# Head totals in a decoder layer: a rounded part and a remainder in place of full fp32 operands

## The chip, the cores and the metric

The kernel runs on one NeuronCore of a Trainium2 chip. The metric is the device time of one execution in microseconds (us). The engines work side by side and meet at semaphores: TensorE (PE) multiplies and writes PSUM banks, VectorE (DVE) and ScalarE (ACT) do elementwise work, GpSimd (POOL) and SyncE (SP) mostly start DMA transfers. Each engine takes its instructions in the order in which they are written, so whatever stands behind a wait on its engine waits too.

## What is computed

One inference step of one decoder layer for 256 prompt tokens and 8 requests of 4 tokens each, 288 token columns in all. The part that the change touches is the RWKV-7 branch, cut to its core:

```
kk = heads(k * k_k)
kk = kk * rsqrt(max(sum(kk * kk, axis=-1), 1e-24))              # total over a head of 64 channels
... S = S * w + (S a) b + v k  per token, y = S r ...
mean = mean(y, axis=-1)                                          # total over a head
var  = mean(square(y - mean), axis=-1)                           # total over a head
y = (y - mean) * rsqrt(var + GN_EPS) * lnx_w + lnx_b
bonus = sum(r_h * k_h * r_k, axis=-1) * v_h                      # total over a head
out = (y + bonus) * g
```

Around it stand the large products `n @ w_in`, the gates, `p_rw`, `p_att`, `w_o`, `w_up` and `w_down`, all in fp32.

## The kernel before

**The stream.** Nearly all of TensorE's time goes to the large products. Their weights come in units of 16 blocks (a block is a 128x128 tile of weights, a unit is 1 MB, loaded by one DMA). To reach fp32 accuracy each weight tile is made into a rounded part `w_hi` (a ScalarE copy to the type fp32r) and a remainder `w_lo` (a VectorE subtraction), and the activations into `x_split` in the same way. A block is then three matmuls of 128x288: `w_lo` by the activations' rounded part (L621), `w_hi` by their remainder (L622), `w_hi` by their rounded part (L623). A unit n may start when the semaphore `w_split` says that its `w_lo` is done and `unit_out` says that the bank of the unit before last is read.

**The pairs.** The 16 heads are done two at a time in 8 pairs (a loop over 7 and a last one that is written out). A pair is a chain of small fp32 matmuls with VectorE and ScalarE steps between them. Where TensorE would have to wait for such a step, `fill(count)` puts in so many blocks of the gate weights. A pair has four units, 64 blocks, to fill with; `fill` counts them on, and the first block of each unit waits for that unit's `w_lo`. In order, a pair takes 39 blocks up to the point at which y is made, and the tail of a pair is this:

```python
                mm(BK[5][:, 0:N], head_ones, YS[:], start=True, stop=True).then_inc(sem("y_mean"), 1)
                if not last:
                    kk_sum(it + 2)
                fill(4)
                pe.wait_ge(sem("y_sq"), v)
                mm(BK[5][:, 0:N], head_ones, YQ[:], start=True, stop=True).then_inc(sem("y_var"), 1)
                if not last:
                    log_decay(it + 2)
                fill(6)
                if not last:
                    bonus_mm(it + 2)
                fill(KT * 4 - pos[0])
```

The pair's first three units use up blocks 0 to 47; block 48, the first of the fourth unit, lies in `fill(6)`. `head_ones` is a 128x128 matrix that adds the 64 channels of each of the two heads. Four totals use it, each as one fp32 matmul of 128x288: the mean of y (L1116), its variance (L1121), and for the next pair the norm of kk (`kk_sum`, L862) and the bonus (`bonus_mm`, L875).

**VectorE in the tail.** In written order: the last states `state(c)`, the grown request state (L2253), the copy of y for the requests (L2256), `mix_prev` for v, the request state by its decay (L2262), y less its mean (L2265), `kk_max` (L2046), two quarters of the fourth unit's `w_lo` (L579), `k_mixed` for the next pair (L2062, L2063), the other two quarters (L579; the last one raises `w_split`), then `head` for the next pair: a reciprocal (L2074) and ten short steps up to `ar_ready`, which TensorE waits for at the start of the next pair (L905), and last the `w_lo` of the next pair's first unit (L567).

**The last pair** has no next pair to prepare: after its four `w_lo` quarters VectorE goes on with the reciprocal of the standard deviation (L2108), the norm, the gate, the `w_lo` of the first unit of the projection, and `o_split` (L2306), for which TensorE waits at the projection's first block.

**Ahead of the pairs** the same steps stand once for pair 0, with `fill_cols` in the place of `fill`: `kk_square` on ScalarE (L1459), `kk_sum(1)`, `log_decay(1)`, `bonus_mm(1)`. On VectorE `streamed(FILL_FIRST)`, the `w_lo` of a unit, stands ahead of `kk_max(1)`.

**The start.** `first_units` begins with four units in step, a quarter of each at a time. The first blocks need quarter 0 of the first unit as `w_hi` (L1258) and `w_lo` (L1777), and the first activations as rounded part (L1247) and remainder (L1769).

## Time and profile before

| | |
|---|---|
| time of three runs | 1776.01, 1778.01, 1780.81 us; median 1778.01 |
| the profiled execution | 1776.88 us, its span 1775.3 us |
| mean granted TensorE clock | 0.996 of full |
| TensorE busy | 1758.8 us, 99% of the span |
| VectorE busy | 1120.7 us, 63% |
| ScalarE busy | 759.6 us, 43% |
| the pairs | from about 360 us to 711 us |

Times in the views are microseconds from the start of the span. A row of a timeline has the start, the time up to the end of the last one, the engine, the line, the operation, its output and inputs, and how many instructions were merged; in brackets stands the idle time just before and what ended it. PEld is the load of a weight tile, which goes on beside the matmuls. Matmuls are pipelined: one row's time is that from its start to its modelled end, and the pace is the distance between starts. An fp32 matmul stands as two records, one of the fp32r type as one record.

### The profile page before, as it was taken

The page shows a single profiled execution, that of the slowest core. Times are in us where ns is not written, and L with a number is a line of the kernel's source. Part 1 is how long each engine was busy: PE and PEld are TensorE (multiplying, and loading weights), DVE is VectorE, ACT ScalarE, POOL GpSimd, SP SyncE. Part 2 cuts the span into 40 slices and gives each one's busy share as a digit, 9 for nine tenths or more (in the row PEclk, how much of TensorE's full clock was granted, in tenths as well). Part 3 has the DMA queues.
Part 4 walks back from the last instruction along what each step waited for, and adds up shares of the span by engine and source line. Part 5 has one row for each costly group of instructions (what it writes and reads, how often), then busy time and mean ns, then how long its engine had stood idle before and what let it go on. Part 6 is the DMA issues. An engine that isn't in the chain of part 4 may idle for free.

```text
span 1775.3 us, 40657 instructions
## 1 busy us (share of the span) xinstructions
PE 1758.8 (99%) x16482; PEld 1708.2 (96%) x16482; DVE 1120.7 (63%) x2015; ACT 759.6 (43%) x1059; POOL 53.8 (3%) x103
## 2 busy tenths in 40 slices
PE   9999999999999999999999999999999999999997
PEld 9999899999999998999999999999999999999997
DVE  7764864667777777665566666666666665444443
ACT  6456444555555554333443333333333333333332
POOL 2500000000000000000000000000000000000000
PEclk9999999999999999999999999999999999999998
DMA  7644344433333332644454444444444444555553
GB/s 285 220 165 165 124 162 157 143 115 118 112 112 117 112 111 103 220 166 170 171 220 163 157 164 158 168 161 167 164 165 165 165 165 167 172 169 175 170 169 134
DMA packets 51697, 283.47 MB, mean 160 GB/s; under 512 B 7248, under 2 KB 11856, under 8 KB 25776
## 3 DMA queue, kind: packets, MB, share of 16 engines
q1 hardware_dynamic: 43488, 260.32, 41.9%
q10 hardware_dynamic: 3888, 12.59, 1.9%
q0 software_dynamic: 4256, 9.65, 1.8%
q8 instruction: 46, 0.75, 0.2%
q14 instruction: 19, 0.16, 0.0%
HBM read 274.26 MB, written 8.27 MB: 159 GB/s over the span
## 4 chain that ended last, share of the span: by engine, by line
PE 96%; DVE 3%; DMA 0%; ACT 0%; issue 0%; DVEq 0%; ACTq 0%
PE bank L621 30%; PE bank L623 28%; PE bank L622 28%; PE bank L945 1%; PE bank L985 1%; DVE w_lo L567 1%; DVE scores L1939 1%; PE bank L642 0%; PE bank L643 0%; PE bank L644 0%; DMA w_raw<-in_w_in 0%; PE bank L905 0%; DVE max L1906 0%; PE bank L852 0%; PE bank L800 0%; PE bank L817 0%
## 5 line engine op out<-in xcount | busy, mean ns | idle before, releaser
L621 PE MATMUL bank<-x_split,w_lo 128*128 128x288 f32 x2880 | 872.8, 303 | 2.8 <-DVE w_lo L567 2.1
L622 PE MATMUL bank<-x_split,w_hi 128*128 128x288 f32 x2880 | 849.6, 295 | 0.0
L623 PE MATMUL bank<-x_split,w_hi 128*128 128x288 f32 x2880 | 847.2, 294 | 0.0
L587 ACT ACTIVATE w_hi<-w_raw 128x2048 fp32r<-128x2048 f32 (+1 forms) x262 | 468.7, 1789 | 591.8 <-PE bank L623 579.1
L567 DVE TENSOR_TENSOR w_lo<-w_raw,w_hi 128x2048 fp32r<-128x2048 f32 (+1 forms) x238 | 503.8, 2117 | 283.2 <-ACT w_hi L587 282.9
L621 PEld LDWEIGHTS bank<-x_split,w_lo 128*128 128x128 f32 x2880 | 540.3, 188 | 18.0 <-issue 8.2
L622 PEld LDWEIGHTS bank<-x_split,w_hi 128*128 128x128 f32 x2880 | 541.0, 188 | 2.6 <-issue 1.5
L623 PEld LDWEIGHTS bank<-x_split,w_hi 128*128 128x128 f32 x2880 | 542.2, 188 | 0.0
L621 PE MATMUL bank<-act_split,w_lo 128*128 128x288 f32 x704 | 208.5, 296 | 0.0
L622 PE MATMUL bank<-act_split,w_hi 128*128 128x288 f32 x704 | 207.7, 295 | 0.0
L623 PE MATMUL bank<-act_split,w_hi 128*128 128x288 f32 x704 | 207.0, 294 | 0.0
L623 PEld LDWEIGHTS bank<-act_split,w_hi 128*128 128x128 f32 x704 | 132.6, 188 | 0.0
L622 PEld LDWEIGHTS bank<-act_split,w_hi 128*128 128x128 f32 x704 | 132.2, 188 | 0.0
L621 PEld LDWEIGHTS bank<-act_split,w_lo 128*128 128x128 f32 x704 | 131.9, 187 | 0.2 <-DVE w_lo L567 0.2
L621 PE MATMUL bank<-merged_split,w_lo 128*128 128x288 f32 x256 | 75.9, 296 | 0.0
L622 PE MATMUL bank<-merged_split,w_hi 128*128 128x288 f32 x256 | 75.5, 295 | 0.0
L623 PE MATMUL bank<-merged_split,w_hi 128*128 128x288 f32 x256 | 75.3, 294 | 0.0
L2397 DVE TENSOR_TENSOR conv<-bank,h_rstd 128x288 f32<-128x288 f32 x44 | 20.2, 458 | 67.9 <-PE bank L623 67.9
L579 DVE TENSOR_TENSOR w_lo<-w_raw,w_hi 128x512 fp32r<-128x512 f32 x96 | 62.1, 683 | 1.1
L1320 ACT ACTIVATE cols<-bank 128x256 f32<-128x256 f32 x40 | 15.4, 385 | 90.5 <-PE bank L623 90.5
L2380 DVE TENSOR_TENSOR gate_ext<-bank,h_rstd 128x256 f32<-128x256 f32 x44 | 18.7, 425 | 55.0 <-PE bank L623 55.0
L623 PEld LDWEIGHTS bank<-merged_split,w_hi 128*128 128x128 f32 x256 | 48.2, 188 | 0.0
(396 smaller groups left out, 1544.2 us busy)
## 6 DMA issues: line engine op xcount, KB each, us to landing
w_raw<-in_w_up SPq DMA_DIRECT2D x88, 1024.0 KB, 4.8
w_raw<-in_w_in SPq DMA_DIRECT2D x47, 1024.0 KB, 4.9
w_raw<-in_w_down SPq DMA_DIRECT2D x64, 704.0 KB, 4.1
w_raw<-in_w_gate SPq DMA_DIRECT2D x32, 1024.0 KB, 4.8
w_raw<-in_w_p SPq DMA_DIRECT2D x16, 1024.0 KB, 4.9
w_raw<-in_w_o SPq DMA_DIRECT2D x16, 1024.0 KB, 4.8
h<-in_x ACTq DMA_DIRECT2D x1, 2304.0 KB, 11.2
h_spill<-h ACTq DMA_DIRECT2D x1, 2304.0 KB, 9.3
```

Source lines behind the costliest of these rows:

```text
L567: eng.tensor_tensor(WLO[:, slot, 0:kt], WRAW[:, slot, 0:kt], WHI[:, slot, 0:kt].bitcast(F32), ALU.subtract).then_inc(sem("w_split"), 1)
L579: ins = dve.tensor_tensor(WLO[:, slot, k], WRAW[:, slot, k], WHI[:, slot, k].bitcast(F32), ALU.subtract)
L587: actv(WHI[:, slot, 0:kt], WRAW[:, slot, 0:kt], ACT.Copy).then_inc(sem("w_hi"), 3 if isinstance(n, int) and n == 2 else 1)
L621: mm(out, wl, hi, start=first and k == ks[0], stop=False, skip_group_check=True)
L622: mm(out, w, lo, start=False, stop=False, skip_group_check=True)
L623: ins = mm(out, w, hi, start=False, stop=last and k == ks[-1], skip_group_check=True)
L945: ins = mm(BK[bank][q, u * w:(u + 1) * w], lhs[q, u], rhs[q, u], start=True, stop=True)
L985: return mm(BK[banks[par]][halves[e], c0:c0 + CH], lhs, rhs, start=start, stop=False, skip_group_check=True)
L1320: actv(tile[:, 1:1 + SEQ], BK[j % 2][:, 0:SEQ], ACT.Copy)
L1939: ins = V.scalar_tensor_tensor(acc, src, w, acc if i or par else causal[qt], ALU.mult, ALU.add)
L2380: V.tensor_tensor(gx[:, 2:2 + SEQ], BK[0][:, 0:SEQ], HRSTD[:, 0:SEQ], ALU.mult)
L2397: st.done(V.tensor_tensor(c[:, 0:N], BK[1][:, 0:N], HRSTD[:], ALU.mult))
```

## The change

- Each of the four totals is made by `head_sum` from two fp32r matmuls, the remainder first, then the rounded part, with a ones matrix `HONES` of the type fp32r. The operands are new: `SQS` (squares of k), `YSS` (y, and then its squares) and `RKS` (the bonus product).
- The rounded parts of the squares of k, of y and of its squares are made on ScalarE by a second activation; their remainders on VectorE by a subtraction. Both parts of the bonus product are made on VectorE, a copy (CAST) and a subtraction.
- In the tail of a pair `kk_sum` goes ahead of the mean, and `fill(4)` and `fill(6)` become `fill(6)` and `fill(5)`.
- VectorE: the grown request state goes ahead of the state of chunk 3; `kk_lo` stands behind that state, and in the part ahead of the pairs it stands ahead of `streamed(FILL_FIRST)`. The map of chunk 3 becomes a tile of its own, 128x64.
- At the start the first unit's first two blocks put the products with `w_hi` first and those with `w_lo` after them, and the first two activations are made ahead of the weights.

```diff
--- before.py
+++ after.py
@@ -390,3 +390,5 @@
     LO = m("l_off", [P, 2, 2 * BL])
-    MTB = m("chunk_map", [P, NCH - 1, P])
+    HONES = m("head_ones_r", [P, P], F32R)
+    MTB = m("chunk_map", [P, NCH - 2, P])
+    MT3 = m("chunk_map_3", [P, CH])
     MLS = region(vv_at)("m_low_s", [NS, 2, NS])
@@ -859,5 +874,10 @@
 
+            def head_sum(bank, split):
+
+                mm(BK[bank][:, 0:N], HONES[:], split[:, 1, :], start=True, stop=False, skip_group_check=True)
+                return mm(BK[bank][:, 0:N], HONES[:], split[:, 0, :], start=False, stop=True, skip_group_check=True)
+
             def kk_sum(v):
-                pe.wait_ge(sem("kk_sq"), v)
-                mm(BK[3][:, 0:N], head_ones, SQK[:], start=True, stop=True).then_inc(sem("kk_sum"), 1)
+                pe.wait_ge(sem("kk_sq"), 2 * v)
+                head_sum(3, SQS).then_inc(sem("kk_sum"), 1)
 
@@ -1113,13 +1133,13 @@
 
-                pe.wait_ge(sem("y"), v)
-                pe.wait_ge(sem("y_cols"), v)
-                mm(BK[5][:, 0:N], head_ones, YS[:], start=True, stop=True).then_inc(sem("y_mean"), 1)
                 if not last:
+                    pe.wait_ge(sem("y_cols"), 2 * v - 1)
                     kk_sum(it + 2)
-                fill(4)
-                pe.wait_ge(sem("y_sq"), v)
-                mm(BK[5][:, 0:N], head_ones, YQ[:], start=True, stop=True).then_inc(sem("y_var"), 1)
+                pe.wait_ge(sem("y"), 3 * v - 1)
+                head_sum(5, YSS).then_inc(sem("y_mean"), 1)
+                fill(6)
+                pe.wait_ge(sem("y"), 3 * v)
+                head_sum(5, YSS).then_inc(sem("y_var"), 1)
                 if not last:
                     log_decay(it + 2)
-                fill(6)
+                fill(5)
                 if not last:
@@ -1261,5 +1281,5 @@
             actv(ROOT[:, 0:1], NORMS[:, 0, 0:1], ACT.Copy)
+            first_hi(0, 2, "x_in0")
             act.wait_ge(sem("w_first_in"), 16)
             first_weights(0, [0])
-            first_hi(0, 2, "x_in0")
             first_hi(2, 4, "x_in0b")
@@ -1458,3 +1478,5 @@
                 act.wait_ge(sem("rkv"), v)
-                actv(SQK[:], RKV[:, 1, :], ACT.Square, scale=PRM[:, PR_KK:PR_KK + 1]).then_inc(sem("kk_sq"), 1)
+                for dst in (SQK[:], SQS[:, 0, :]):
+                    ins = actv(dst, RKV[:, 1, :], ACT.Square, scale=PRM[:, PR_KK:PR_KK + 1])
+                ins.then_inc(sem("kk_sq"), 1)
 
@@ -1544,2 +1566,5 @@
                 ins.then_inc(sem("y_cols"), 1)
+                act.wait_ge(sem("y"), 3 * v - 2)
+                act.wait_ge(sem("y_cols"), 2 * v - 1)
+                actv(YSS[:, 0, :], YS[:], ACT.Copy).then_inc(sem("y_cols"), 1)
                 if not last:
@@ -1548,3 +1573,5 @@
                 act.wait_ge(sem("y_centred"), v)
-                actv(YQ[:], YS[:], ACT.Square).then_inc(sem("y_sq"), 1)
+                for dst in (YQ[:], YSS[:, 0, :]):
+                    ins = actv(dst, YS[:], ACT.Square)
+                ins.then_inc(sem("y_sq"), 1)
                 if not last:
@@ -1806,5 +1833,6 @@
 
-            first_weights(0, [0])
             dve.wait_ge(sem("norms_in"), 16)
-            first_lo(0, 4)
+            first_lo(0, 2)
+            first_weights(0, [0])
+            first_lo(2, 4)
             first_weights(0, [1, 2, 3])
@@ -2043,2 +2071,7 @@
 
+            def kk_lo(v):
+
+                dve.wait_ge(sem("kk_sq"), 2 * v - 1)
+                V.tensor_tensor(SQS[:, 1, :], SQK[:], SQS[:, 0, :].bitcast(F32), ALU.subtract).then_inc(sem("kk_sq"), 1)
+
             def kk_max(v):
@@ -2062,4 +2095,5 @@
                 st.done(V.scalar_tensor_tensor(KP[:], KP[:], 1.0, RKV[:, 1, :], ALU.add, ALU.mult))
-                V.scalar_tensor_tensor(RKR[:], RKV[:, 0, :], PRM[:, PR_RK:PR_RK + 1], KP[:], ALU.mult,
-                                       ALU.mult).then_inc(sem("rkr"), 1)
+                st.done(V.scalar_tensor_tensor(RKR[:], RKV[:, 0, :], PRM[:, PR_RK:PR_RK + 1], KP[:], ALU.mult, ALU.mult))
+                st.done(V.tensor_copy(RKS[:, 0, :], RKR[:]))
+                V.tensor_tensor(RKS[:, 1, :], RKR[:], RKS[:, 0, :].bitcast(F32), ALU.subtract).then_inc(sem("rkr"), 1)
 
@@ -2230,8 +2264,6 @@
                 state(0)
-                for e, h in enumerate(halves):
-                    V.tensor_tensor(MTB[h, 0::2, e * HD:(e + 1) * HD], BK[7][h, P:2 * P].rearrange("p (u f) -> p u f", u=2),
-                                    spread(eye_ch[h], 1, [CH, 2, CH]), ALU.add)
-                for e, h in enumerate(halves):
-                    ins = V.tensor_tensor(MTB[h, 1, e * HD:(e + 1) * HD], BK[6][h, P + CH:2 * P], eye_ch[h], ALU.add)
-                ins.then_inc(sem("map"), 1)
+                for c, src in ((1, BK[7][:, P:P + CH]), (2, BK[6][:, P + CH:2 * P])):
+                    for e, h in enumerate(halves):
+                        V.tensor_tensor(MTB[h, c - 1, e * HD:(e + 1) * HD], src[h], eye_ch[h], ALU.add)
+                V.tensor_tensor(MT3[:], BK[7][:, P + CH:2 * P], eye_ch, ALU.add).then_inc(sem("map"), 1)
                 rv = AR[:, 1, :].rearrange("p (c f) -> p c f", f=CH)
@@ -2247,9 +2279,12 @@
                         mix_prev(it + 1, 0)
+                    if c == 3:
+                        dve.wait_ge(sem("state_s_mm"), v)
+                        for r in range(2):
+                            half = SIN[:, 4 * r:4 * r + 4, :]
+                            ins = V.tensor_tensor(half, half, BK[(5, 2)[r]][:, 0:256].rearrange("p (b f) -> p b f", f=HD), ALU.add)
+                        ins.then_inc(sem("s_grown"), 1)
                     dve.wait_ge(sem("state_mm"), v * 3 - 3 + c)
                     state(c)
-                dve.wait_ge(sem("state_s_mm"), v)
-                for r in range(2):
-                    half = SIN[:, 4 * r:4 * r + 4, :]
-                    ins = V.tensor_tensor(half, half, BK[(5, 2)[r]][:, 0:256].rearrange("p (b f) -> p b f", f=HD), ALU.add)
-                ins.then_inc(sem("s_grown"), 1)
+                if not last:
+                    kk_lo(it + 2)
                 dve.wait_ge(sem("y_mm"), v)
@@ -2260,5 +2295,7 @@
                     dve.sem_inc(sem("v_mixed"), 1)
+                dve.wait_ge(sem("y_cols"), 2 * v)
+                V.tensor_tensor(YSS[:, 1, :], YS[:], YSS[:, 0, :].bitcast(F32), ALU.subtract).then_inc(sem("y"), 1)
                 dve.wait_ge(sem("s_grown"), v)
                 V.tensor_tensor(SIN[:], SIN[:], spread(PC[:, NCH:], 2, [P, DB, HD]), ALU.mult).then_inc(sem("state_s_done"), 1)
-                dve.wait_ge(sem("y"), v)
+                dve.wait_ge(sem("y"), 3 * v - 1)
                 dve.wait_ge(sem("y_mean"), v)
@@ -2267,2 +2304,4 @@
                     kk_max(it + 2)
+                dve.wait_ge(sem("y_sq"), v)
+                V.tensor_tensor(YSS[:, 1, :], YQ[:], YSS[:, 0, :].bitcast(F32), ALU.subtract).then_inc(sem("y"), 1)
                 for part in range(2):
@@ -2285,2 +2324,4 @@
             dve.sem_inc(sem("v_mixed"), 1)
+            st.done(V.tensor_copy(HONES[:], head_ones))
+            kk_lo(1)
             streamed(FILL_FIRST)
```

**TensorE, tail of a pair.** `bank<-y,main_consts` is a head total of before; `bank<-y_split,head_ones_r` is one of the two matmuls of a total of the change, and `waits` names the semaphores of a row. Left out ("...") are only rows of blocks. Before:

```order
L1116 MATMUL bank<-y,main_consts 128x288 [waits y_cols,y]
L862 MATMUL bank<-squares_k,main_consts 128x288 [waits kk_sq]
...
L1121 MATMUL bank<-y_sq,main_consts 128x288 [waits y_sq]
L870 MATMUL bank<-main_consts,decay_tok 128x130 [waits g_sb,decay_tok]
...
L887 REGISTER_ALU
L621 MATMUL bank<-x_split,w_lo 128x288 [waits unit_out,w_split]
...
L875 MATMUL bank<-r_k_rk,main_consts 128x288 [waits rkr]
```

With the change:

```order
L881 REGISTER_ALU [waits y_cols]
L877 MATMUL bank<-squares_k_split,head_ones_r 128x288 [waits kk_sq]
L878 MATMUL bank<-squares_k_split,head_ones_r 128x288
...
L877 MATMUL bank<-y_split,head_ones_r 128x288 [waits y]
...
L890 MATMUL bank<-main_consts,decay_tok 128x130 [waits g_sb,decay_tok]
...
L907 REGISTER_ALU
L627 MATMUL bank<-x_split,w_lo 128x288 [waits unit_out,w_split]
...
L877 MATMUL bank<-r_k_rk_split,head_ones_r 128x288 [waits rkr]
```

Between the mean and the row that waits for `w_split` (block 48) stood nine blocks and stand nine blocks (four and five before, six and three now), with the variance and `log_decay` two blocks later among them. Behind that row one block stood ahead of the bonus, and two stand there now.

**VectorE, tail of a pair**, from the copy of y to the reciprocal of the next pair's head. Before:

```order
L2256 COPY y<-bank 128x32 [waits y_mm]
...
L2262 TENSOR_TENSOR state_s<-state_s,chunk_decay 128x512 [waits dve_step,s_grown]
L2265 SCALAR_TENSOR_TENSOR y<-bank,y 128x288 [waits y_mean,y]
L2046 TENSOR_SCALAR squares_k<-bank 128x288 [waits kk_sum]
L579 TENSOR_TENSOR w_lo<-w_raw,w_hi 128x512 [waits w_hi]
L579 TENSOR_TENSOR w_lo<-w_raw,w_hi 128x512
L2062 SCALAR_TENSOR_TENSOR k_mixed<-k_mixed,rkv 128x288 [waits k_part,rkv]
L2063 SCALAR_TENSOR_TENSOR r_k_rk<-rkv,pair_params,k_mixed 128x288 [waits dve_step]
L579 TENSOR_TENSOR w_lo<-w_raw,w_hi 128x512 x2
L2074 RECIPROCAL squares_k<-squares_k 128x288 [waits kk_norm]
```

With the change:

```order
L2302 SCALAR_TENSOR_TENSOR y<-bank,y 128x288 [waits y_mean,y]
L2079 TENSOR_SCALAR squares_k<-bank 128x288 [waits kk_sum]
L2306 TENSOR_TENSOR y_split<-y_sq,y_split 128x288 [waits y_sq]
L585 TENSOR_TENSOR w_lo<-w_raw,w_hi 128x512 [waits w_hi]
L585 TENSOR_TENSOR w_lo<-w_raw,w_hi 128x512
L2095 SCALAR_TENSOR_TENSOR k_mixed<-k_mixed,rkv 128x288 [waits k_part,rkv]
L2096 SCALAR_TENSOR_TENSOR r_k_rk<-rkv,pair_params,k_mixed 128x288 [waits dve_step]
L2097 CAST r_k_rk_split<-r_k_rk 128x288 [waits dve_step]
L2098 TENSOR_TENSOR r_k_rk_split<-r_k_rk,r_k_rk_split 128x288 [waits dve_step]
L585 TENSOR_TENSOR w_lo<-w_raw,w_hi 128x512 x2
L2108 RECIPROCAL squares_k<-squares_k 128x288 [waits kk_norm]
```

A subtraction that waits for ScalarE's squares now stands ahead of the first two quarters of `w_lo`, and a copy and a subtraction, each behind a wait of VectorE for itself, ahead of the last two.

## Rows read from the trace of the kernel before

**Rows 1.** The page's first part: busy time, share of span, instructions.

```profile
PE 1758.8 (99%) x16482; PEld 1708.2 (96%) x16482; DVE 1120.7 (63%) x2015; ACT 759.6 (43%) x1059; POOL 53.8 (3%) x103
```

**Rows 2.** Windows: length, busy time and instructions of PE, PEld, DVE, ACT, POOL; PEclk.

```profile
11.00:12.80 1.80, 1.80 (x7) 1.80 (x8) 1.80 (x4) 1.80 (x5) 0.00 (x0) 0.50 0.93 383
391.00:435.10 44.10, 44.10 (x746) 39.79 (x745) 35.15 (x93) 23.20 (x50) 2.20 (x4) 1.00 0.32 113
1000.00:1700.00 700.00, 700.00 (x5250) 699.77 (x5249) 401.44 (x606) 252.85 (x225) 0.00 (x0) 1.00 0.48 166
```

**Rows 3.** Timeline of TensorE in the tail of a pair.

```profile
391.28 0.65 PE L1116 MATMUL bank<-y,main_consts 128*128 128x288 f32 x2
...
391.76 0.65 PE L862 MATMUL bank<-squares_k,main_consts 128*128 128x288 f32 x2
...
393.84 0.65 PE L1121 MATMUL bank<-y_sq,main_consts 128*128 128x288 f32 x2
...
396.99 0.30 PE L621 MATMUL bank<-x_split,w_lo 128*128 128x288 f32 x1
...
403.87 0.38 PE L905 MATMUL bank<-main_consts,b_t 128*128 128x128 f32 x2
```

**Rows 4.** Timeline of VectorE in the same tail.

```profile
392.04 0.46 DVE L2265 SCALAR_TENSOR_TENSOR y<-bank,y 128x288 f32<-128x288 f32 x1 [1.14 <-PE bank L1116]
...
392.82 1.28 DVE L579 TENSOR_TENSOR w_lo<-w_raw,w_hi 128x512 fp32r<-128x512 f32 x2
...
394.51 0.52 DVE L2063 SCALAR_TENSOR_TENSOR r_k_rk<-rkv,pair_params,k_mixed 128x288 f32<-128x288 f32 x1
394.95 1.29 DVE L579 TENSOR_TENSOR w_lo<-w_raw,w_hi 128x512 fp32r<-128x512 f32 x2
...
398.32 0.52 DVE L2075 SCALAR_TENSOR_TENSOR kk_unit<-rkv,pair_params,squares_k 128x288 f32<-128x288 f32 x1
398.88 0.46 DVE L2076 SCALAR_TENSOR_TENSOR a_gate<-a_gate,kk_unit 128x288 f32<-128x288 f32 x1
...
400.79 0.42 DVE L2102 TENSOR_TENSOR k_t<-k_mixed,decay_exp 128x256 f32<-128x256 f32 x1
```

**Rows 5.** Timeline of ScalarE in the same tail.

```profile
392.53 0.44 ACT L1549 ACTIVATE y_sq<-y 128x288 f32<-128x288 f32 x1 [0.55 <-DVE y L2265]
392.88 0.51 ACT L1450 ACTIVATE decay_tok<-decay_tok 128x384 f32<-128x384 f32 x1
```

**Rows 6.** Groups of instructions by shape (count, busy us, mean ns), VectorE.

```profile
L2032 DVE TENSOR_SCALAR cols<-cols 128x288 f32<-128x288 f32 x1 | 0.3, 311 | 0.0
```

**Rows 7.** Timelines of the part ahead of the pairs.

```profile
341.28 0.53 ACT L1459 ACTIVATE squares_k<-rkv,pair_params 128x288 f32<-128x288 f32 x1
341.42 2.29 DVE L567 TENSOR_TENSOR w_lo<-w_raw,w_hi 128x2048 fp32r<-128x2048 f32 x1 [0.21 <-ACT w_hi L587]
350.13 2.28 DVE L567 TENSOR_TENSOR w_lo<-w_raw,w_hi 128x2048 fp32r<-128x2048 f32 x1
342.10 0.65 PE L862 MATMUL bank<-squares_k,main_consts 128*128 128x288 f32 x2
353.29 0.30 PE L621 MATMUL bank<-x_split,w_lo 128*128 128x288 f32 x1
```

**Rows 8.** Timeline of the last pair's tail.

```profile
698.88 0.45 ACT L1543 ACTIVATE y<-bank 128x128 f32<-128x128 f32 x2 [1.72 <-PE bank L985]
699.66 0.72 PE L1116 MATMUL bank<-y,main_consts 128*128 128x288 f32 x2
700.86 2.48 DVE L579 TENSOR_TENSOR w_lo<-w_raw,w_hi 128x512 fp32r<-128x512 f32 x4
710.88 0.37 PE L621 MATMUL bank<-x_split,w_lo 128*128 128x288 f32 x1
```

**Rows 9.** Timeline of TensorE at the start.

```profile
8.43 0.37 PE L642 MATMUL bank<-x_split,w_lo 128*128 128x288 f32 x1 [1.84 <-DVE x_split L1769]
...
10.99 0.61 PE L642 MATMUL bank<-x_split,w_lo 128*128 128x288 f32 x1 [0.28 <-DVE w_lo L1777]
```

More of the change, by code:

```diff
@@ L191 @@
 ATT_STEPS = [("sample", 0), (0, 0), (0, 1), (1, 0), (1, 1), ("sample", 1)]
-PAIR_STEPS = 16
+PAIR_STEPS = 18
 TOKEN_TILES = (0, P, N - P)
@@ L398, in build @@
     RKR = m("r_k_rk", [P, N])
+    RKS = m("r_k_rk_split", [P, 2, N], F32R)
+    YSS = m("y_split", [P, 2, N], F32R)
+    assert m.at <= inv_at + 3 * size_of([P, 4, CH])
+    SQS = region(r0)("squares_k_split", [P, 2, N], F32R)
     m = region(big)
@@ L631, in first_units @@
                     for u in range(FIRST):
+                        out = BK[first_bank(u)][:, 0:N]
+                        if s == 0 and u == 0:
+                            pe.wait_ge(sem("w_part_hi"), 1)
+                            for k in range(2):
+                                pe.wait_ge(sem("x_split"), k + 1)
+                                mm(out, WHI[:, 0, k], XN[:, 0, k], start=k == 0, stop=False, skip_group_check=True)
+                                mm(out, WHI[:, 0, k], XN[:, 1, k], start=False, stop=False, skip_group_check=True)
                         if s < 2 and u < 3:
@@ L635, in first_units @@
                             pe.wait_ge(sem("w_split"), s + 1)
-                        out = BK[first_bank(u)][:, 0:N]
-                        for k in range(4):
+                        if s == 0 and u == 0:
+                            for k in range(2):
+                                mm(out, WLO[:, 0, k], XN[:, 0, k], start=False, stop=False, skip_group_check=True)
+                        for k in range(2 if s == 0 and u == 0 else 0, 4):
                             t = 4 * s + k
@@ L874, in bonus_mm @@
                 pe.wait_ge(sem("rkr"), v)
-                mm(BK[4][:, 0:N], head_ones, RKR[:], start=True, stop=True).then_inc(sem("bonus_mm"), 1)
+                head_sum(4, RKS).then_inc(sem("bonus_mm"), 1)
             def pair(it, last=False):
@@ L1097, in pair @@
                 for e, h in enumerate(halves):
-                    ins = grown(grow, 0, 1, MTB[h, 2, e * HD:(e + 1) * HD], ST[h, 2, :], e, 1)
+                    ins = grown(grow, 0, 1, MT3[h], ST[h, 2, :], e, 1)
                 ins.then_inc(sem("state_mm"), 1)
```

2 lines of the change are left out of this document (1 added, 1 removed).

## The prediction

> **What bounds the kernel now.** I read the page first: TensorE is busy 99% of the span [rows 1], so time is won only where it gets less to do, and lost wherever it waits. The windows come next. In the pure stream it starts 5250 matmuls in 700 us, 0.133 us each, 0.40 us a block; in a pair it is busy through the whole window, while VectorE has 35.15 and ScalarE 23.20 of 44.10 us [rows 2]. A pair takes (699.66 - 391.28) / 7 = 44.05 us from one mean to the next [rows 3, 8]. So the share of busy time says that VectorE has room, but the question is where in the pair it has it. For that I read the three engines' timelines over the tail of a pair [rows 3 to 5]: block 48 starts at 396.99 us, and the last quarter of its `w_lo` ends at 394.95 + 1.29 = 396.24 us. The fourth unit has 0.75 us to spare, much less than the average suggests.
>
> **What TensorE saves.** A total in fp32 takes 391.76 - 391.28 = 0.48 us [rows 3]. Two fp32r matmuls of the same shape at the stream's pace take 2 x 0.133 = 0.27 us. Each total saves 0.21 us; four in a pair save 0.86 us and two in the last pair 0.43 us. All blocks are done in either order, and the map of chunk 3 keeps the shape of its matmuls: nothing there.
>
> **When TensorE reaches block 48.** Nine blocks lie between the mean and block 48 in both kernels, and three totals besides: 396.99 - 3 x 0.21 = 396.35 us. The other 0.21 us is saved by the bonus, behind it.
>
> **When the `w_lo` of block 48 is ready.** I follow VectorE, on the clock of the same tail.
> - The mean now follows the norm of kk and ends with a short matmul: starts 391.55 and 391.68, end 0.30 later, 391.97, against about 391.93 before. L2265 starts at 392.08 instead of 392.04 [rows 4].
> - ScalarE squares y at 392.57. Its next activation could start 392.88 - 392.53 = 0.35 us later [rows 5], so the second square runs from 392.92 and takes 0.44: 393.36. VectorE has by then ended `kk_max` (392.08 + 0.37 + 0.46 = 392.91) and stands still. At 393.40 it makes the remainder. A VectorE instruction on 128x288 lasts 0.46 us and lets the next start some 0.09 us ahead of its end: the quarters start at 393.77, 0.95 us later than the 392.82 of before [rows 4].
> - L2063 starts 394.51 - 392.82 = 1.69 us after the first quarter: 395.46. The next quarters came 0.44 us after that. Now the copy has to wait until L2063 has written, and L2075 to L2076 shows what such a wait makes of a 0.52 us instruction: 0.56 us [rows 4]. Copy and subtraction follow: 0.35 + 0.37. The last two quarters start at 395.46 + 0.56 + 0.35 + 0.37 = 396.74 and end at 398.03. TensorE goes on at 398.08.
> - The copy's 0.31 us is that of L2032, a one-input instruction of this width from SBUF to SBUF [rows 6]. It is the nearest row. The upper bound is the 0.46 us of L2265, 0.15 us more a pair; nothing of this width is below L2032.
>
> The Trainium skill ("VectorE: DVE Perf Modes") says that fp32 instructions with one SBUF input can run at twice the rate of those with two, and the 0.31 against 0.46 us agree with it; it does not say whether writing fp32r keeps this. By the one the forecast would stand, by the other it would be 1 us higher.
>
> **So TensorE waits 398.08 - 396.35 = 1.73 us at block 48**, a wait that does not exist now, and 0.86 us of it is paid by the shorter totals: **+0.87 us a pair**, 7 pairs, **+6.1 us**. With the copy at 0.46, with 0.1 more for ScalarE's hand-over, it is 1.1 a pair (7.7 us); with 0.1 us less than I count, 0.75 (5.3 us). Behind the wait on TensorE stand two blocks, the bonus, and the rest of the unit. The bonus needs the remainder of its operand, ready at about 396.8: hidden by the wait at block 48; without it, TensorE would reach the bonus near 397.1 and still not wait. The head of the next pair shifts by about 1.7 us on VectorE, but TensorE reaches L905 at 403.87 + 0.87 = 404.74, and `ar_ready`, raised at 400.79 + 0.42 = 401.21 before [rows 4], is there at 402.9. The `w_lo` behind it takes 2.3 us [rows 7] and ends about 405.5; the block that needs it stands behind all transposes and the first products of the next pair. ScalarE is 0.35 us later and has idle time in each pair [rows 2].
>
> **Hidden edits.** `kk_lo` and y's remainder (0.46 us each) fall into the 1.14 us in which VectorE waited for the mean [rows 4]. `kk_lo` hangs on ScalarE's two squares and y's remainder on ScalarE's copy; both have a good microsecond until the matmuls that read them at 391.28 and 391.55. The grown request state moves into a gap ahead of the last state. The map costs VectorE one short instruction more, about 0.1 us, under two blocks of stream. Without these covers each would cost at most its own length a pair.
>
> **The last pair.** It has no norm of kk or LoRA products ahead of its mean as cover. ScalarE has y at 698.88 + 0.45 = 699.33; a rounded part (0.44) and a remainder (0.45) more with their hand-overs: 700.30, and TensorE, there at 699.66, waits until 700.35. The mean is then short, and L2265 starts about 0.42 us later than before. Two squares and the remainder put the four quarters at 702.60 instead of 700.86, and what VectorE does next (reciprocal, norm, gate, `w_lo`, `o_split`) goes on 1.74 us later. TensorE reaches the projection's first block about 0.85 us later than before and finds it not ready: it starts at 710.88 + 1.74 [rows 8]. **+1.7 us** (0.85 if the first block of the projection hangs on TensorE alone now, to 2.0).
>
> **Ahead of the pairs.** ScalarE squares k at 341.28; with a second square it ends at about 342.22, VectorE's remainder at 342.71. TensorE reaches the total at 342.10 [rows 7] and waits 0.66 us for it. The `w_lo` behind `kk_lo` starts 1.2 us later, and with the copy and subtraction of the bonus (0.79) the `w_lo` of 350.13 + 2.28 = 352.41 ends at 354.40 instead. Its unit starts at 353.29 [rows 7], now 353.29 + 0.66 - 0.43 = 353.52, and waits 0.9 us. In all **+1.2 us** (0.4 to 1.4).
>
> **The start.** The first four products with `w_hi` run in a stretch in which TensorE waited until 8.43. But the second unit starts when its own `w_lo` is there, at 10.99, as before [rows 9]; the weights come from a DMA that isn't moved. What can be won is the half clock of 1.2 GHz that rows show here (0.50 in 11.0 to 12.8 us [rows 2], after TensorE had stood still for 1.84 us): up to 0.9 us if the clock rises earlier; if it stays low longer through the new gap, 1 us is lost. I take **-0.4 us**.
>
> **Sum.** 6.1 + 1.7 + 1.2 - 0.4 = +8.6 us against the profiled execution's 1776.88 us: 1785.5. That execution is 1.13 us below the median of 1778.01, so I forecast **1786.6 us**, 0.48% slower.
>
> **The rivals.**
> 1. *The stall is short and the sum stays within 0.3%.* For it: the start may give 0.9 us, the copy and hand-overs have bounds of 0.1 us, and the wait ahead of the pairs and in the last pair rests on margins of a few tenths. All low ends together: 5.3 + 0.85 + 0.4 - 0.9 = +5.7; with a pair at 0.65 instead of 0.75, +5: 1783. Against it: five low ends at a time. 0.13.
> 2. *The clock falls at each stall.* A gap of 1.84 us at the start was followed by a stretch at 0.50 of the clock. In its part from 11.0 to 12.8 us TensorE started 7 matmuls, where the stream's pace gives 13.5: 6.5 x 0.133 = 0.9 us lost there, and with what lies ahead of 11.0 I estimate 1.4 us [rows 2, 9]. The new gap in a pair is nearly as long (1.6 to 1.7 us). If it did the same in every pair: 7 x 1.4 = 9.8 more, 1796 us; in two or three pairs, 1790. Against it: TensorE is busy without a gap ahead of it, and at the start it was not. 0.15. The Trainium skill ("TensorE: Matmul & The Clock Gate", HAM oscillation) says that idle gaps in a loop can throw TensorE back to half clock again and again, and this start is such a case; no gap of this length in the middle of a busy stretch is in this trace.
> 3. *The gain comes through: faster.* The totals save 32 x 0.21 = 6.8 us, 1771 us. It decides on one point: the `w_lo` of block 48 must be ready by 396.35. Even without the change it is ready at 396.28, so VectorE may lose no more than 0.07 us ahead of it, and I count 1.8 us: the squares' hand-over 0.95, copy and subtraction 0.84. Only a wrong reading of which unit `fill(5)` enters would do it. 0.04.
> The forecast's own case has 0.68, with a range of 1784 to 1790.
>
> **Numbers.** A measurement of this kernel tells about 0.3% (5.3 us) from no change, so slower by more than that begins at 1783.3. Slower has the forecast's case and rival 2, 0.82 with a little of their low ends taken off; within 0.3% 0.14; faster 0.04. The range leaves out the gain and the clock falling in every pair, and takes in part of rivals 1 and 2: 1782 to 1793 us.
>
> **What the changed profile would show.** TensorE's waits: a row for blocks of the stream, released by VectorE's `w_lo` quarters, some 1.6 us long and seven times; none in the pairs would refute me. In the timeline two records 0.13 us apart for each total, and the wait three blocks behind `log_decay`, two ahead of the bonus; at any other block I have misread its place. VectorE idle 0.45 us ahead of the remainder of y's squares. Mean to mean 44.9 us instead of 44.05. The first block of the projection near 1.7 us later after the last mean. What would make me wrong is a copy or a hand-over much shorter than its bounds, a clock below 1.00 in the pairs' windows, or a second wait in the pair that I hold to be covered, at L905 above all.

## The result and the profile after

| kernel | median us | range, runs | ratio to before [95%] |
|---|---|---|---|
| before | 1776.57 | 1776.01 to 1780.81, 7 | |
| changed | 1785.54 | 1784.27 to 1788.55, 7 | 1.0052 [1.0042, 1.0061] |

The change costs 8.97 us, 0.52%. The profiled execution of the changed kernel took 1788.55 us (span 1787.0), 3.0 us above its own median; most of these 3 us lie at the start, as told below.

The chain of reading is the same as before the change: the page first, then the list of waits, then the timelines of the tail. The page of the changed kernel, first part and the group of the stream's `w_lo` blocks (the last two numbers are the idle time ahead of the group and what ended most of it):

```profile
PE 1754.4 (98%) x16482; PEld 1704.2 (95%) x16482; DVE 1136.7 (64%) x2064; ACT 768.5 (43%) x1083; POOL 53.8 (3%) x103
...
L627 PE MATMUL bank<-x_split,w_lo 128*128 128x288 f32 x2880 | 870.1, 302 | 15.7 <-DVE w_lo L585 11.5
```

TensorE is busy 4.4 us less than in [rows 1] and yet the span is 11.7 us longer: it stands still. The waits of TensorE say where (waited in total, times, longest, us):

```profile
PE bank L627 <- DVE w_lo L585: 11.5, 8, 1.6
...
PE bank L657 <- DVE w_lo L573: 1.8, 1, 1.8
PE bank L643 <- ACT w_hi L1278: 1.7, 1, 1.7
PE bank L627 <- DVE x_split L2347: 0.7, 1, 0.7
PE bank L877 <- DVE squares_k_split L2075: 0.6, 1, 0.6
PE bank L877 <- DVE y_split L2297: 0.6, 1, 0.6
```

Its first row is the forecast wait at block 48: 7 times 1.57 us, and 0.48 us once in the last pair. TensorE's timeline in the tail of a pair, against [rows 3]:

```profile
394.37 0.51 PE L877 MATMUL bank<-squares_k_split,head_ones_r 128*128 128x288 f32 x1
394.72 0.30 PE L878 MATMUL bank<-squares_k_split,head_ones_r 128*128 128x288 f32 x1
394.86 0.29 PE L877 MATMUL bank<-y_split,head_ones_r 128*128 128x288 f32 x1
...
399.25 0.29 PE L627 MATMUL bank<-x_split,w_lo 128*128 128x288 f32 x1
...
401.38 0.40 PE L627 MATMUL bank<-x_split,w_lo 128*128 128x288 f32 x1 [1.57 <-DVE w_lo L585]
...
401.89 0.29 PE L627 MATMUL bank<-x_split,w_lo 128*128 128x288 f32 x1
...
402.28 0.30 PE L877 MATMUL bank<-r_k_rk_split,head_ones_r 128*128 128x288 f32 x1
...
665.50 0.29 PE L877 MATMUL bank<-y_split,head_ones_r 128*128 128x288 f32 x1
```

The block at 399.25 is the last of the third unit. A block takes 0.40 us, so block 48 would have started at 399.65; it starts at 401.38, 1.73 us later. (The view's 1.57 is counted from the modelled end of the block before. By starts each wait is 0.16 us longer than the view says, and starts are what adds up.) From the first mean to the seventh are (665.50 - 394.86) / 6 = 45.11 us. Two blocks behind the wait the bonus follows without one. The block behind the wait takes longer: its successor starts at 401.89, 0.51 us later and not 0.40.

VectorE's timeline of the same tail, against [rows 4], and the two squares of ScalarE:

```profile
395.40 0.46 DVE L2302 SCALAR_TENSOR_TENSOR y<-bank,y 128x288 f32<-128x288 f32 x1 [0.78 <-PE bank L878]
395.77 0.45 DVE L2079 TENSOR_SCALAR squares_k<-bank 128x288 f32<-128x288 f32 x1
396.70 0.46 DVE L2306 TENSOR_TENSOR y_split<-y_sq,y_split 128x288 fp32r<-128x288 f32 x1 [0.48 <-ACT y_split L1575]
397.07 1.29 DVE L585 TENSOR_TENSOR w_lo<-w_raw,w_hi 128x512 fp32r<-128x512 f32 x2
398.77 0.52 DVE L2096 SCALAR_TENSOR_TENSOR r_k_rk<-rkv,pair_params,k_mixed 128x288 f32<-128x288 f32 x1
399.32 0.31 DVE L2097 CAST r_k_rk_split<-r_k_rk 128x288 fp32r<-128x288 f32 x1
399.66 0.46 DVE L2098 TENSOR_TENSOR r_k_rk_split<-r_k_rk,r_k_rk_split 128x288 fp32r<-128x288 f32 x1
400.04 1.29 DVE L585 TENSOR_TENSOR w_lo<-w_raw,w_hi 128x512 fp32r<-128x512 f32 x2
```

```profile
395.89 0.45 ACT L1575 ACTIVATE y_sq<-y 128x288 f32<-128x288 f32 x1 [0.60 <-DVE y L2302]
396.24 0.43 ACT L1575 ACTIVATE y_split<-y 128x288 fp32r<-128x288 f32 x1
```

Before the change the first pair of quarters started 0.78 us behind the centring (392.82 - 392.04 in [rows 4]); now 397.07 - 395.40 = 1.67. From the first pair of quarters to the second were 2.13 us; now 400.04 - 397.07 = 2.97. So the handover of the squares costs 0.89 us and the split of the bonus's operand 0.84 us (2.97 - 2.13). The last quarter ends at 401.33, and TensorE goes on 0.05 us later.

The windows, as in [rows 2] (length, busy time and instructions of PE, PEld, DVE, ACT, POOL; PEclk is the number behind POOL's):

```profile
394.86:440.08 45.22, 43.65 (x748) 39.53 (x747) 37.07 (x99) 24.46 (x54) 2.20 (x4) 1.00 0.32 110
400.00:404.00 4.00, 2.62 (x19) 2.62 (x20) 3.93 (x6) 3.99 (x8) 0.00 (x0) 1.00 0.63 208
11.00:12.80 1.80, 1.80 (x15) 1.80 (x14) 1.80 (x5) 1.63 (x4) 0.00 (x0) 1.00 1.00 392
```

VectorE is busy 37.07 of 45.22 us, 82%, in a pair in which TensorE waits for it. The clock of the pairs is 1.00, also in the 4 us around the wait. At the start it is 1.00 where [rows 2] have 0.50. But it falls later. These windows lie ahead of and behind the wait of 1.84 us that ends at 23.60 us (its row stands below):

```profile
10.80:21.70 10.90, 10.90 (x83) 10.72 (x81) 6.98 (x15) 7.76 (x15) 0.00 (x0) 1.00 0.94 338
25.00:28.00 3.00, 3.00 (x14) 3.00 (x14) 2.49 (x3) 3.00 (x4) 0.00 (x0) 0.50 0.85 339
```

TensorE was busy without a gap for more than 10 us, stood for 1.84 us, and about 1.3 us after it went on it ran at 0.50 for some 3 us: 13 matmuls at 0.24 us and not 0.133, 1.4 us lost on top of the wait.

The part ahead of the pairs, the last pair and the start, against [rows 7], [rows 8] and [rows 9], TensorE and (for `y`) ScalarE:

```profile
344.89 0.40 PE L877 MATMUL bank<-squares_k_split,head_ones_r 128*128 128x288 f32 x1 [0.59 <-DVE squares_k_split L2075]
356.57 0.40 PE L627 MATMUL bank<-x_split,w_lo 128*128 128x288 f32 x1 [0.65 <-DVE w_lo L573]
```

```profile
708.78 0.45 ACT L1565 ACTIVATE y<-bank 128x128 f32<-128x128 f32 x2 [1.83 <-PE bank L1005]
710.31 0.41 PE L877 MATMUL bank<-y_split,head_ones_r 128*128 128x288 f32 x1 [0.58 <-DVE y_split L2297]
722.56 0.37 PE L627 MATMUL bank<-x_split,w_lo 128*128 128x288 f32 x1 [0.71 <-DVE x_split L2347]
```

```profile
10.30 0.40 PE L657 MATMUL bank<-x_split,w_lo 128*128 128x288 f32 x1 [0.61 <-DVE w_lo L1804]
23.60 0.40 PE L657 MATMUL bank<-x_split,w_lo 128*128 128x288 f32 x1 [1.84 <-DVE w_lo L573]
```

Ahead of the pairs the total of k's squares waits 0.59 us for its remainder, and the unit at 356.57 0.65 us for its `w_lo`. In the last pair 722.56 - 708.78 = 13.78 us lie between ScalarE's y and the projection's first block, where [rows 8] give 710.88 - 698.88 = 12.00: +1.78. At the start the second unit begins 0.69 us earlier than in [rows 9], at full clock; at 23.60 TensorE then stands for 1.84 us.

What start and preparation cost together is read from two landmarks of TensorE, one behind the start and one ahead of the first norm and mean in the loop. Before:

```profile
71.67 0.38 PE L662 MATMUL bank<-main_consts,cols 128*128 128x128 f32 x2
390.79 0.65 PE L858 MATMUL bank<-cols,lora 128*128 128x288 f32 x2
```

With the change:

```profile
73.68 0.38 PE L677 MATMUL bank<-main_consts,cols 128*128 128x128 f32 x2
394.10 0.65 PE L873 MATMUL bank<-cols,lora 128*128 128x288 f32 x2
```

The first is 2.01 us later, the second 3.31.

### The profile page after: what moved, and what is told of

Its sections match the earlier page's. It is cut to its first block, busy times and chain, and to the rows that moved or that the text cites. A ratio compares the mean times of both kernels' runs of the same rounds, so it can differ in the third digit from the quotient of the medians.

```text
span 1787.0 us, 40776 instructions
## 1 busy us (share of the span) xinstructions
PE 1754.4 (98%) x16482; PEld 1704.2 (95%) x16482; DVE 1136.7 (64%) x2064; ACT 768.5 (43%) x1083; POOL 53.8 (3%) x103
## 4 chain that ended last, share of the span: by engine, by line
PE 91%; DVE 6%; issue 1%; ACT 1%; DMA 1%; DVEq 0%; ACTq 0%
PE bank L627 29%; PE bank L629 27%; PE bank L628 27%; PE bank L965 1%; DVE w_lo L573 1%; PE bank L1005 1%; DVE w_lo L585 1%; DVE scores L1967 1%; DMA w_raw<-in_w_in 1%; PE bank L925 0%; DVE max L1934 0%; PE bank L867 0%; PE bank L815 0%; PE bank L832 0%; PE bank L657 0%
## 5 line engine op out<-in xcount | busy, mean ns | idle before, releaser
L627 PE MATMUL bank<-x_split,w_lo 128*128 128x288 f32 x2880 | 870.1, 302 | 15.7 <-DVE w_lo L585 11.5
L593 ACT ACTIVATE w_hi<-w_raw 128x2048 fp32r<-128x2048 f32 (+1 forms) x262 | 468.9, 1790 | 595.1 <-PE bank L629 583.9
```

What stands on the lines that cost most here:

```text
L593: actv(WHI[:, slot, 0:kt], WRAW[:, slot, 0:kt], ACT.Copy).then_inc(sem("w_hi"), 3 if isinstance(n, int) and n == 2 else 1)
L627: mm(out, wl, hi, start=first and k == ks[0], stop=False, skip_group_check=True)
```

## The experiments

Each is timed against the kernel before. a_order, a_bonus, a_squares and b_start ran on one chip (before: 1776.26 us, 29 runs), the others on a second one (1776.11, 18 runs). No runs of the changed kernel stand beside them, so a difference between two of these kernels, or to the changed kernel's 1785.54 us, rests on the kernel before as the common measure; the ratios say how well. "Pair" is the distance between the second and the third execution of ScalarE's y copy in the profile: 44.19 us before (432.98 to 477.17), 45.11 in the changed kernel (437.26 to 482.37).

| kernel | median us (range, runs) | ratio [95%] | pair us | wait at block 48, us |
|---|---|---|---|---|
| a_order | 1775.63 (1774.68 to 1778.34, 11) | 0.9999 [0.9990, 1.0008] | 43.72 | none |
| a_bonus | 1780.99 (1780.29 to 1783.20, 7) | 1.0031 [1.0019, 1.0042] | 44.48 | 0.73 |
| a_squares | 1778.52 (1777.61 to 1780.30, 11) | 1.0013 [1.0004, 1.0022] | 44.21 | 0.46 |
| b_start | 1776.74 (1774.36 to 1777.72, 11) | 1.0001 [0.9992, 1.0010] | 44.18 | none |
| a_ends | 1782.87 (1781.90 to 1783.26, 5) | 1.0037 [1.0024, 1.0050] | 45.09 | 1.57 |
| a_nostart | 1786.59 (1785.07 to 1787.41, 5) | 1.0055 [1.0043, 1.0068] | 45.11 | 1.57 |
| c_fill | 1772.85 (1771.64 to 1777.59, 12) | 0.9982 [0.9974, 0.9991] | 43.34 | none |
| c_ends | 1770.55 (1769.42 to 1771.57, 6) | 0.9966 [0.9955, 0.9978] | 43.34 | none |

**a_order** moves only VectorE's work in the pair: the quarters of the fourth unit ahead of the squares' remainder (one of them ahead of its wait) and ahead of the bonus's operand.

```diff
-                dve.wait_ge(sem("y_sq"), v)
-                V.tensor_tensor(YSS[:, 1, :], YQ[:], ...).then_inc(sem("y"), 1)
-                for part in range(2):
-                    split_part(dve, n + 3, 1, part)
-                if not last:
-                    k_mixed(it + 2)
-                for part in range(2, 4):
-                    split_part(dve, n + 3, 1, part)
+                split_part(dve, n + 3, 1, 0)
+                dve.wait_ge(sem("y_sq"), v)
+                V.tensor_tensor(YSS[:, 1, :], YQ[:], ...).then_inc(sem("y"), 1)
+                for part in range(1, 4):
+                    split_part(dve, n + 3, 1, part)
+                if not last:
+                    k_mixed(it + 2)
```

> The changed kernel with one move on VectorE: in the tail of a pair one quarter of the fourth unit's w_lo goes ahead of the remainder of y's squares, and the other three go ahead of k_mixed, so that all four stand ahead of the bonus product's copy and subtraction. No work is added or left out. If the loss is the wait for that w_lo at block 48 (my theory): the quarters end near 395.7 on the clock of the prediction, TensorE comes at 396.35, the wait of 1.6 us a pair goes, and a wait of about 0.3 us at the bonus takes its place; 7 x 1.3 and 0.6 in the last pair: about 10 us less than the changed kernel, near 1775.5. If the loss is the added work as such, or a slower clock or slower matmuls of the head totals, wherever VectorE does it (rival): within 1 us of the changed kernel's 1785.5.

All operations are still there, and 9.9 us of the time are gone (9.4 by the ratios, 1.0052 less 0.9999). The wait at block 48 has left the list; in its place stands a short one of the bonus for its remainder. The row of the list of waits, and the same wait in TensorE's timeline with the last block ahead of it:

```profile
PE bank L877 <- DVE r_k_rk_split L2098: 1.4, 7, 0.2
```

```profile
398.01 0.29 PE L627 MATMUL bank<-x_split,w_lo 128*128 128x288 f32 x1
...
398.77 0.40 PE L877 MATMUL bank<-r_k_rk_split,head_ones_r 128*128 128x288 f32 x1 [0.20 <-DVE r_k_rk_split L2098]
```

By starts it is 398.77 - (398.01 + 0.40) = 0.36 us. The pair should be 0.86 shorter and 0.36 longer than 44.19, 43.69; it is 43.72. With the same work on VectorE and the same two squares on ScalarE the stall at block 48 is gone: it came from what stood ahead of the `w_lo` quarters, not from the sum of the work. The kernel is only level with the one before, since the bonus waits now and the parts outside the loop still lose.

**a_bonus** takes the bonus back to one fp32 matmul; the copy and the subtraction are left out on VectorE.

```diff
-                head_sum(4, RKS).then_inc(sem("bonus_mm"), 1)
+                mm(BK[4][:, 0:N], head_ones, RKR[:], start=True, stop=True).then_inc(sem("bonus_mm"), 1)
...
-                st.done(V.tensor_copy(RKS[:, 0, :], RKR[:]))
-                V.tensor_tensor(RKS[:, 1, :], RKR[:], RKS[:, 0, :].bitcast(F32), ALU.subtract).then_inc(sem("rkr"), 1)
```

> The changed kernel with the bonus total alone back in fp32 (no copy and no subtraction on VectorE for it). By my theory VectorE's last two quarters come 0.79 us earlier, the wait at block 48 falls from 1.6 to 0.8 us, and the fp32 total behind it costs 0.21: 7 x -0.58 = -4.1, and -0.4 ahead of the pairs: near 1781. By the rival, that TensorE's own time is all that counts, it gets 8 x 0.21 = 1.7 us slower: 1787.

```profile
PE bank L627 <- DVE w_lo L585: 5.6, 8, 0.7
```

The wait falls by 1.57 - 0.73 = 0.84 us, the whole price of the split as forecast, and the pair is 0.63 us shorter than the change's: 0.84 less the 0.21 that the bonus now costs TensorE again. The time, 1780.99 us, is that of the theory (1781) and not that of the rival (1787).

**a_squares** takes the total of y's squares back: one square on ScalarE, no remainder on VectorE, one fp32 matmul.

```diff
-                pe.wait_ge(sem("y"), 3 * v)
-                head_sum(5, YSS).then_inc(sem("y_var"), 1)
+                pe.wait_ge(sem("y_sq"), v)
+                mm(BK[5][:, 0:N], head_ones, YQ[:], start=True, stop=True).then_inc(sem("y_var"), 1)
...
-                dve.wait_ge(sem("y_sq"), v)
-                V.tensor_tensor(YSS[:, 1, :], YQ[:], YSS[:, 0, :].bitcast(F32), ALU.subtract).then_inc(sem("y"), 1)
```

> The changed kernel with the variance alone back in fp32 (one square on ScalarE, no remainder on VectorE). By my theory the quarters come 0.95 us earlier and TensorE comes 0.21 us later to block 48: wait 0.45 us instead of 1.6, net -0.95 a pair, -6.6, and -1.0 in the last pair, where the chain of VectorE sets the start of the projection: near 1778. By the rival that TensorE's own time is all that counts: 8 x 0.21 slower, 1787.

The wait is 0.46 us, seven times (0.47 once). By starts it is 0.62, and the three totals that stay short pay 3 x 0.21: the pair is 44.21 us, that of before. The 2.3 us that the kernel still loses lie outside the looped pairs: 1.3 ahead of them, and 1.0 in the last pair, where 13.01 us lie between ScalarE's y and the projection, against 12.00.

**b_start** is the kernel before with the change's start alone; **a_nostart** is the change with the start of before.

```diff
-            act.wait_ge(sem("w_first_in"), 16)
-            first_weights(0, [0])
             first_hi(0, 2, "x_in0")
+            act.wait_ge(sem("w_first_in"), 16)
+            first_weights(0, [0])
...
-            first_weights(0, [0])
             dve.wait_ge(sem("norms_in"), 16)
-            first_lo(0, 4)
+            first_lo(0, 2)
+            first_weights(0, [0])
+            first_lo(2, 4)
```

and on TensorE the first unit's products with `w_hi` of its first two blocks ahead of those with `w_lo`.

> The kernel before with the change of the start alone. I forecast -0.4 us (from -0.9 to +1.0) for it: the second unit is bound by its weights, and only the half clock at 9.7 to 12.8 us can be won. In the profile of the changed kernel the stretch ran at full clock, but TensorE then waited 1.8 us at 23.6 us for the third quarter's w_lo, whose weights had come late. If that late landing belongs to the changed start, this kernel is 1 to 2 us slower than before; if it is chance, it is within 0.5 us.

> The changed kernel with the start as it was before. The start alone, on the kernel before, was within 0.5 us, since TensorE gets 1.6 us ahead and then waits for the third quarter's w_lo. So 1785.5 within 1 us. If the late landing seen in the changed profile is typical for the changed start, this is 2 us faster: 1783.5.

The windows of both (a_nostart, then b_start), and the waits of TensorE ahead of the first unit and in it:

```profile
9.70:12.80 3.10, 3.10 (x14) 3.10 (x14) 3.10 (x7) 2.85 (x8) 0.00 (x0) 0.50 0.97 403
```

```profile
9.70:12.80 3.10, 2.47 (x19) 2.24 (x18) 2.74 (x6) 3.07 (x7) 0.00 (x0) 1.00 0.95 398
```

```profile
PE bank L648 <- DVE x_split L1787: 1.8, 1, 1.8
```

```profile
PE bank L637 <- ACT w_hi L1267: 1.1, 1, 1.1
```

The clock follows the start: 0.50 with the old order and its gap of 1.8 us, 1.00 with the new one, whose gap (1.1 us in b_start) lies earlier. The other seven kernels with the new start show 1.00 in this window as well. The times do not: b_start's interval spans 0.9 in 1000 either way, 1.6 us, and those of a_nostart and of the change overlap. Neither the forecast 0.4 us nor zero is excluded. a_nostart was expected within 1 us of the changed kernel's 1785.54 and came 1.05 above it.

The traces show what decides it. TensorE's lead from the full clock lasts until it wants the third quarter's `w_lo` near 23 us, and that hangs on when the weights have landed. ScalarE's first rounding of that quarter began at 17.29 us before, at 17.50 in b_start, 18.43 in a_nostart, 18.64 in a_order and 19.30 in the changed kernel:

```profile
19.30 1.92 ACT L593 ACTIVATE w_hi<-w_raw 128x2048 fp32r<-128x2048 f32 x1 [2.96 <-issue]
```

The load of this quarter was issued at 12.17 us before and took 5.0 us to land; in the changed kernel it was issued earlier, at 11.48, and took 7.8. Over all ten kernels it was issued between 11.3 and 12.2 us and took 5.0 to 7.8 us. TensorE waited for the quarter 1.84 us in the changed kernel, 1.1 in a_order, and not at all in b_start and a_nostart.

The landmark behind the start (L662 and its like, 71.67 us before) says what each start was worth in its one profiled execution:

| start | kernel: rounding of the third quarter from, landmark (us) |
|---|---|
| old | before: 17.29, 71.67; a_nostart: 18.43, 71.48 |
| new, landed early | b_start: 17.50, 70.58; a_squares: 17.78, 70.81; a_ends: 17.84, 70.89 |
| new, later | a_bonus: 18.16, 72.41; c_ends: 18.40, 71.43; a_order: 18.64, 71.68; changed: 19.30, 73.68; c_fill: 19.71, 72.75 |

With early weights the new start gives 0.8 to 1.1 us against 71.67; with later ones the outcome lies between a gain of 0.2 and a loss of 2.0. The mean of the eight is 71.78 us: nothing is left on average that one could tell from zero. Landing is not all of it. a_bonus waits 0.65 us more for `squares` at 33.45. The changed kernel is the only one of the eight whose clock fell behind its wait. From the end of that wait to the landmark it takes 73.68 - 23.60 = 50.08 us; a_order takes 71.68 - 22.93 = 48.75 and c_fill 72.75 - 24.01 = 48.74, with waits of 1.10 and 1.60 us and a clock of 1.00 behind them. So the fall of the clock cost 1.3 us.

**a_ends** is the change with the plain fp32 total in the three places that have no cover: the first norm of kk and the first bonus, ahead of the pairs, and mean and variance of the last pair.

```diff
-            kk_sum(1)
+            kk_sum(1, True)          # one fp32 matmul, no rounded part
...
+                if last:
+                    mm(BK[5][:, 0:N], head_ones, YS[:], ...)
+                    fill(4)
+                    pe.wait_ge(sem("y_sq"), v)
+                    mm(BK[5][:, 0:N], head_ones, YQ[:], ...)
```

> The changed kernel with the two places outside the seven looped pairs as they were before: the norm and the bonus of pair 0 and the mean and the variance of the last pair are fp32 totals again, without splits. By my terms this gives back 1.3 us ahead of the pairs and 1.8 us in the last pair (the changed profile shows 1.30 and 1.78): 3.1 us less than the changed kernel, near 1782.4. If a wait there was cover for something that comes later anyway (rival), nothing or less than 1 us.

```profile
PE bank L627 <- DVE w_lo L585: 11.0, 7, 1.6
```

Only the seven waits of the pairs are left; 6.8 us above before is what is left, against 6.4 from the pair's length (7 x 0.92). The kernel is 2.7 us below the changed one, where 3.1 were expected.

**c_fill** is a_order with one block more of the stream ahead of the bonus, and **c_ends** is c_fill with the edits of a_ends.

```diff
-                fill(5)
+                fill(6)
                 if not last:
                     bonus_mm(it + 2)
```

> The version with the w_lo quarters ahead of the bonus split, and one block more ahead of the bonus, which there was 0.20 us late in each pair. If nothing else ends later, 7 x 0.2 = 1.4 us less than that version's 1775.6: 1774.2. If the next pair's head is what binds next (rival), no gain.

> The same, and pair 0's and the last pair's totals in fp32 as in the kernel before. Twenty-eight short totals are left (4 in each of 7 tails), 28 x 0.21 = 6.0 us of TensorE's time, with every wait of mine gone: near 1776.3 - 6.0 = 1770.5, and 2.5 to 3 us less than the version without this. If the looped pairs keep a wait of 0.2 us, 1772.

The wait at the bonus is gone from the list in both; its two matmuls stand 0.21 us apart and not 0.13, which leaves 0.08 us a pair. c_fill gained 2.8 us over a_order where 1.4 was expected: I had read 0.2 us a pair from the idle view, and the 0.36 by starts is what a wait costs; the pair went from 43.72 to 43.34 us, and 7 x 0.38 = 2.7. c_ends, expected at 1770.5 us, came at 1770.55, 2.3 below c_fill (2.5 to 3 expected). It has all four totals short in the looped pairs, where there is cover, and plain ones elsewhere. Its pair is 44.19 - 43.34 = 0.85 us shorter, about four times 0.21, and it is 0.34% faster than before.

## Why the prediction was right, point by point

| term | forecast us | measured us | from |
|---|---|---|---|
| wait at block 48, by starts | 1.73 | 1.73 | timeline |
| a looped pair | +0.87 | +0.92 | 45.11 - 44.19 |
| seven pairs | +6.1 | +6.4 | |
| last pair | +1.7 | +1.78 | timeline |
| ahead of the pairs | +1.2 | +1.30 | below |
| start, profiled execution | -0.4 | +2.01 | below |
| start, by the medians | -0.4 | about -0.5, not resolved | 8.97 less the others |
| changed less before | +8.6 | +8.97 | medians |
| time of the changed kernel | 1786.6 | 1785.54 | median |

- **The place and size of the wait.** It is at block 48, three blocks behind `log_decay`, seven times. Its parts were right too: the squares' handover 0.91 forecast (0.95 with the 0.04 us by which the centring was to start later) and 0.89 found, copy and subtraction 0.84 and 0.84. The copy took 0.31 us, as long as the nearest row with an fp32 output. This agrees with the Trainium skill ("VectorE: DVE Perf Modes", the mode that uses both read ports), here with an output of the type fp32r.
- **The savings.** Two records 0.13 us apart stand for each total, and c_ends shows the 0.85 us of four of them when nothing takes them back. The first fp32r matmul behind an fp32 product (394.37) lasts 0.51 us, but the next starts 0.35 later, and the pair's length shows nothing of it.
- **The pair's length.** The text took 44.05 us from mean to mean and so forecast 44.9. The 44.05 divides by seven a stretch whose last part, the last pair, is shorter; in the loop it is 44.19 (the y copies at 432.98 and 477.17), and 45.11 is 0.92 above that. The difference of the two kernels was not touched by it. The prediction leaves two small terms out: the restart behind a wait (0.51 us for a block and not 0.40) costs 0.11, and the LoRA products ahead of the norm take 0.67 us and not 0.73 in all eight kernels with the new totals, for a reason that was not looked for. 1.73 - 0.86 + 0.11 - 0.06 = 0.92, the measured length; the same sum gives the pairs of a_order, a_bonus and a_squares within 0.02.
- **The last pair.** Right within 0.1 us. TensorE's waits are 0.58 us at the mean, 0.48 at the fourth unit and 0.71 at the projection. The prediction names the first and the last; the middle one is not named in it.
- **Ahead of the pairs.** Sum and parts were right within 0.1 us: by starts, as the forecast counts, the total waits 0.75 us (0.66 forecast) and its unit 0.81 (0.9). The landmark ahead of the first norm in the loop went from 390.79 to 394.10 us, +3.31; of these 2.01 come from the start, 1.30 are left.
- **The start** is the term that the prediction did not see through. The clock is full earlier, and with early weights the gain of up to 1.1 us is that of its bound (0.9). But the text asked only what the second unit wins and not what takes the lead away: the `w_lo` of the third quarter, 13 us later. In the profiled execution its weights were ready 2 us later than before, TensorE waited 1.84 us, the clock fell behind that wait (1.3 us), and the start cost 2.01, outside the +1.0 that the text allowed. The four terms of that execution make 2.01 + 1.30 + 6.4 + 1.78 = 11.5 of the 11.7 us between the spans. By the medians what is left for the start is a gain of about half a microsecond, which no run here resolves; that the forecast of -0.4 meets it is luck as much as working.
- **The level.** The forecast of 1786.6 us stands on a median of three runs of the kernel before, 1778.01; that of seven is 1776.57, 1.44 lower. So the level came 1.1 us high although the difference was forecast 0.4 low.
- **The hidden edits** were never taken out one by one. What speaks for their price of nothing is that the pair's length is accounted for without them.
- **Rival 1** (a short stall) fell on the wait's size. a_squares is what it would have been: a pair of 44.21.
- **Rival 2** (the clock falls at each stall) did not happen in the pairs: PEclk is 1.00 in a whole pair and around its wait, in spite of the gap of 1.57 us, and the time is far from 1790 us. But the argument that the text holds against it, that TensorE is busy without a gap ahead of the stall, does not carry: in this same execution a gap of 1.84 us behind more than 10 busy us was followed by 0.50, at 1.3 us, close to the 1.4 us that the rival asked for. The gap in the pairs is only 0.27 us shorter, and the prediction had nothing to place it on the safe side: that the clock held was partly luck. The Trainium skill ("TensorE: Matmul & The Clock Gate", HAM oscillation) describes the clock falling again and again in a loop that waits for DMA for 3 to 5 us in each round. The gaps that were followed by 0.50 here are shorter than that and came at most once in an execution; the pairs show no such fall, so the rule for a loop is neither confirmed nor refuted.
- **Rival 3** (faster) needed the quarters of block 48 by the time that TensorE comes. a_order gives them that and is level with before (0.9999), as the bonus waits in its place; c_fill has neither wait and is 0.18% faster.

## What to carry to other kernels

Look at the slack of each handover to the bounding engine (here 0.75 us), not at the mean load of the engine that feeds it: VectorE had 18% idle time in a pair and made TensorE wait in each. A shorter operation on the bounding engine is paid for by the preparation of its operands elsewhere; put that preparation behind whatever the bounding engine wants next (here a_order and c_fill), and leave the shorter form out where nothing covers the preparation (ends of loops). Read the length of a wait from starts, check a start-up gain against the next thing that the lead runs into, and look at the granted clock behind every wait, not only in the stretch that the change was made for.

## What was not expected of the hardware

- Ahead of the last 15 us of the kernel, in which TensorE runs out of work, its clock fell to 0.50 three times in the ten profiles, for about 3 us. Each time a gap of 1.82 to 1.84 us lay ahead: in the kernel before and in a_nostart at the start, in the changed kernel at 23.60 us, in the middle of a stretch at 1.00. Shorter gaps left it at 1.00: 1.73 us at the start of the changed kernel, 1.60 in c_fill, 1.57 in each of the seven pairs. A busy stretch ahead of the gap did not protect the clock. Whether the gap's length or something that went along with it decides is not shown: no run varied it alone.
- The load of the third quarter's weights took between 5.0 and 7.8 us in ten profiled executions, and the quarter was ready between 17.3 and 19.7 us. An earlier issue did not bring an earlier landing. That spread is more than most terms of this change, and it goes far to explain why the spans of the two profiles (11.7 us apart) and the medians (8.97) differ.
- A matmul behind a wait was followed by the next after 0.24 us and not 0.13 (401.38 to 401.62 us), at a granted clock of 1.00. So each stop of TensorE costs 0.11 us beyond the wait itself.
